# An expert stage whose blocks run as two loops per expert, with releases of their own, two gather buffers and three kinds of experts

## The reference

```python
logits = h @ w_router + b_router                 # 384 x 32
top_val, top_idx = lax.top_k(logits, 4)
gates = softmax(top_val)
for each expert e, for each block of its rows:   # xb: rows of h that chose e
    hb = xb @ w1[e] + b1[e]                      # 1024 x 2048
    glu, lin = split(hb)
    act = min(glu, 7) * sigmoid(1.702 * min(glu, 7)) * (clip(lin, -7, 7) + 1)
    y = act @ w2[e] + b2[e]                      # 1024 x 1024
    out[rows] += gate * y
```

## Time and profile before

| | |
|---|---|
| median of 3 runs | 1626.13 us |
| the profiled execution's own time | 1619.34 us |
| its span (first to last instruction) | 1617.5 us |
| PE, PEld busy | 85%, 52% |
| DVE, ACT, POOL busy | 37%, 13%, 8% |
| chain that ended last | PE 25%, DMA 23%, SP's queue 9% |
| first block of the experts, end of the span | 601.3 us, 1617.5 us |

### The profile page before, as it was taken

One profiled execution on the slowest core, in us unless ns is written; L12 is line 12 of the kernel. 1 busy time (PEld: TensorE's weight loads), 2 busy tenths in 40 slices (PEclk: granted clock), 3 DMA queues, 4 the chain that ended last, 5 costly groups with the idle time before them and its releaser, 6 DMA issues.

```text
span 1617.5 us, 47273 instructions
## 1 busy us (share of the span) xinstructions
PE 1368.3 (85%) x20097; PEld 843.9 (52%) x20098; DVE 594.4 (37%) x1172; ACT 214.3 (13%) x474; POOL 127.8 (8%) x280
## 2 busy tenths in 40 slices
PE   4899998988978959969778988768968989996965
PEld 1677666777664435525434555435534555552533
DVE  3464644787887552212112221202212221220214
ACT  0332333231302100000000000000000000000001
POOL 1000000000000011101000101001101110110100
PEclk8799999999999979979989999989989999997997
DMA  9656535000116767995999999999999999999992
GB/s 363 204 181 242 185 130 191 2 3 10 54 42 210 291 264 289 419 421 245 419 421 383 420 420 384 422 420 396 410 420 420 387 420 420 383 419 421 387 420 119
DMA packets 88379, 487.56 MB, mean 301 GB/s; under 512 B 13269, under 2 KB 15753, under 8 KB 35609
## 3 DMA queue, kind: packets, MB, share of 16 engines
q1 hardware_dynamic: 81304, 473.59, 72.4%
q10 hardware_dynamic: 3936, 6.69, 1.1%
q0 software_dynamic: 3072, 6.30, 1.1%
HBM read 481.92 MB, written 6.72 MB: 302 GB/s over the span
## 4 chain that ended last, share of the span: by engine, by line
PE 25%; DMA 23%; SPq 9%; DVE 3%; issue 2%; DVEq 0%; POOL 0%; ACT 0%
PE bank L714 25%; DMA work<-w_moe_out 9%; SPq L593 9%; DMA zbuf<-w_moe_out 8%; DMA ring<-w_moe_out 6%; DVE work L2023 1%; DVE work L2025 1%; DVE work L2024 1%; DVE ring L2044 0%; PE bank L710 0%; SPq L596 0%; DVE ring L2049 0%; SPq L628 0%; DVEq L160 0%; SPq L629 0%
## 5 line engine op out<-in xcount | busy, mean ns | idle before, releaser
L714 PE MATMUL bank<-work 128*32 128x256 f32 x5504 | 351.2, 393 | 50.5 <-DMA work<-w_moe_in 31.3
L2019 DVE TENSOR_SCALAR work<-bank 128x256 f32<-128x256 f32 x64 | 40.0, 626 | 736.8 <-PE bank L714 736.8
L714 PE MATMUL bank<-ring,work 128*32 128x256 f32 x3968 | 261.4, 393 | 43.3 <-DMA ring<-w_moe_in 25.9
L714 PEld LDWEIGHTS bank<-work 128*32 128x32 f32 x5504 | 174.0, 113 | 196.0 <-DMA work<-w_moe_in 45.3
L714 PEld LDWEIGHTS bank<-ring,work 128*32 128x32 f32 x3968 | 125.9, 113 | 144.8 <-DMA ring<-w_moe_in 35.1
L714 PE MATMUL bank<-parts 128*128 128x512 f32 (+1 forms) x720 | 168.3, 388 | 2.9 <-DVE parts L446 2.9
L714 PE MATMUL bank<-rowc 32*128 32x256 f32 (+1 forms) x2072 | 142.5, 367 | 22.6 <-issue 22.0
L710 PE MATMUL bank<-work 64*64 64x64 f32 (+3 forms) x3448 | 138.6, 233 | 15.6 <-DVE work L1751 8.5
L714 PEld LDWEIGHTS bank<-parts 128*128 128x128 f32 x720 | 129.3, 191 | 34.1 <-issue 5.2
L710 PEld LDWEIGHTS bank<-work 64*64 64x64 f32 (+2 forms) x3448 | 117.5, 136 | 34.1 <-issue 13.7
L714 PEld LDWEIGHTS bank<-rowc 32*128 32x128 f32 (+1 forms) x2072 | 87.0, 164 | 81.3 <-issue 68.7
(11 more groups left out here) (265 smaller groups left out, 1096.8 us busy)
## 6 DMA issues: line engine op xcount, KB each, us to landing
work<-w_moe_in SPq DMA_DIRECT2D x108, 1024.0 KB, 22.8
ring<-w_moe_in SPq DMA_DIRECT2D x84, 1024.0 KB, 24.9
work<-w_moe_out SPq DMA_DIRECT2D x64, 1024.0 KB, 18.1
ring<-w_moe_out SPq DMA_DIRECT2D x44, 1024.0 KB, 16.7
ring<-w_ada SPq DMA_DIRECT2D x11, 2048.0 KB, 7.5
zbuf<-w_moe_in SPq DMA_DIRECT2D x22, 1024.0 KB
first<-w_moe_in SPq DMA_DIRECT2D x21, 1024.0 KB
spare<-w_moe_in SPq DMA_DIRECT2D x21, 1024.0 KB
```

Of the source, the lines that this page charges most:

```text
L714: return pe.matmul(out, l, r, start=start, stop=stop, skip_group_check=True)
L2019: ts(in_pairs(gl), in_columns(B[0][:, 0:256]), LIMIT, None, ALU.min).then_inc(S["thd"], 1)
```

## The change

- **Two loops per expert.** PE, ACT and DVE run for each expert first `go_in` over its blocks (w1, activation) and then `go_out` (add_up, w2, copy out). On DVE and ACT these stand in a loop over the experts. The activations of an expert's blocks are kept in `zf` (12 slots of 256 columns, `act_of`); `go_out` copies one back into `act` and transposes it.
- **Releases.** w1 chunks count `mult`, w2 chunks count a semaphore of their own, `s_mul2`; SP waits for the one that belongs to the place.
- **Gathers** go into two buffers, one block further ahead. DVE first copies a gathered tile to `xs` and transposes `xT` as soon as PE is done with w1 of the block.
- **Three kinds** of experts: more than two blocks, two blocks, one block, each spread by itself, with the last one-block expert at the end. For these inputs the order becomes 0, 1, 5, 2, 8, 6, 10, 3, 11, 7, 12, 4, 17, 9, 18, 13, 20, 15, 21, 23, 14, 16, 24, 25, 22, 19, 26, 29, 28, 27, 31, 30, with 2, 2, 2, 4, 2, 1, 2, 3, 2, 1, 2, 3, 2, 1, 2, 3, 2, 1, 2, 2, 3, 1, 2, 2, 3, 1, 2, 2, 3, 1, 2, 1 blocks.
- **Small ones.** The table lists the experts of a block by a sum in which one matmul and one copy fall away; 14 small memsets write the addresses of the slots and buffers into it; PE's wait for the full lists moves behind the glu half of the first chunks, and its load of `last_it` goes.

```diff
             def multiplied(used, c):
-                sp.wait_ge(S["mult"], used * WC + (c + 1 - WC + ZQ_ALL))
+                if c < W1C:
+                    sp.wait_ge(S["mult"], used * W1C + (c + 1 - W1C + ZQ_ALL))
+                else:
+                    sp.wait_ge(s_mul2, used * W2C + (c - W1C))
...
-            last_it = gp.value_load(tab[0:1, LAST:LAST + 1], min_val=NE - 1, max_val=NBMAX - 1)
-
-            with gp.Fori(0, last_it) as it:
-                gp.wait_ge(S["xtd"], it + 1)
-                gather_listed(it)
+            last_it = gp.value_load(tab[0:1, LAST:LAST + 1], min_val=NE - 1, max_val=NBUSED - 1)
+
+            gather_listed(1, 1)
+            with gp.Fori(0, last_it + 1, 2) as it:
+                for n in range(2):
+                    gp.wait_ge(S["xtd"], it + (n + 1))
+                    gather_listed(it + (n + 2), n)
+            gp.wait_ge(S["xgd"], 16 * last_it + 48)
...
             pe.wait_ge(S["b3d"], 6)
-            pe.wait_ge(S["idxc"], 2)
-            pe.wait_ge(S["b2d"], 64)
-            last_it = pe.value_load(tab[0:1, LAST:LAST + 1], min_val=NE - 1, max_val=NBMAX - 1)
+            pe.wait_ge(S["b32"], 16 * (NB + 4))
+            pe.wait_ge(S["ohd"], 1)
...
-            def block_of(it, trio, turn_e):
+            def go_in(it, b0, trio, turn_e):
                 pe.wait_ge(S["chos"], it + 1)
+                pe.wait_ge(S["xtd"], it + 1)
                 fours(gb, selw, in_fours(b3[0:QMAX, :], 0), True, False)
-                pe.wait_ge(S["xtd"], it + 1)
...
                     else:
-                        pe.wait_ge(S["yc"], it + 1)
+                        pe.wait_ge(S["idxc"], 2)
+                        pe.wait_ge(S["yc"], b0 + 1)
+                        pe.wait_ge(S["chain2v"], 4 * it + 1)
                         fours(lb, selw, in_fours(b3[0:QMAX, :], 1), True, False)
                     for c in group:
                         fours(lb, xT[:, c, :], in_fours(place_of(turn_e, c), 1), False, c == W1C - 1).then_inc(S["mult"], 1)
+
+            def go_out(it, trio, turn_e):
+                pe.wait_ge(S["yc"], it + 1)
                 pe.wait_ge(S["ohd"], it + 1)
                 add_up(onto, ysb, it + 1)
-                pe.wait_ge(S["actd"], it + 1)
+                pe.wait_ge(S["actd"], it + 2)
                 for c in range(W1C, WC):
                     chunk_landed(trio, turn_e, c)
                     j = W2K[c - W1C]
...
+
+            def blocks_of(e, trio, turn_e):
+                b0, b1 = ended_by(e - 1), ended_by(e)
+                with pe.Fori(b0, b1) as it:
+                    go_in(it, b0, trio, turn_e)
+                with pe.Fori(b0, b1) as it:
+                    go_out(it, trio, turn_e)
 
             def ended_by(e):
-                return pe.value_load(tab[0:1, bass.ds(e + ENDS, 1)], min_val=0, max_val=NBMAX)
+                return pe.value_load(tab[0:1, bass.ds(e + ENDS, 1)], min_val=0, max_val=NBUSED)
 
...
-            add_up(onto, ysb, last_it + 2)
+                    blocks_of(e0 + i, trio, i)
+            blocks_of(NE - 2, 0, NE - 2)
+            blocks_of(NE - 1, 0, NE - 1)
+            end = ended_by(NE - 1)
+            pe.wait_ge(S["yc"], end + 1)
+            pe.wait_ge(S["ohd"], end + 1)
+            add_up(onto, ysb, end + 1)
...
+            sc.sem_inc(s_mul2, 3)
+            sc.sem_inc(S["actd"], 1)
+            sc.sem_inc(S["chain2v"], 1)
...
+            def go_in(it):
+                who = sc.value_load(tab[0:1, bass.ds(it + (WHO + 1), 1)], min_val=0, max_val=NE - 1)
                 sc.wait_ge(S["thd"], 2 * it + 1)
                 sc.activation(th, gl, ACT.Tanh, scale=ALPHA / 2).then_inc(S["thd"], 1)
-                sc.wait_ge(S["mult"], WC * it + (W1C + ZQ_ALL))
-                if not last:
-                    chosen(bass.ds(sc.value_load(tab[0:1, bass.ds(it + (WHO + 1), 1)], min_val=0, max_val=NE - 1), 1))
-                sc.wait_ge(S["mult"], WC * it + (WC + ZQ_ALL))
+                sc.wait_ge(S["mult"], W1C * it + (W1C + ZQ_ALL))
+                chosen(bass.ds(who, 1))
+
+            def go_out(it):
+                sc.wait_ge(s_mul2, W2C * it + (W2C + 3))
                 cp(ysb, B[7][:, 256:512], 0.5).then_inc(S["yc"], 1)
 
-            with sc.Fori(0, last_it) as it:
-                block_of(it, False)
-            block_of(last_it, True)
...
+            for i in range(NACT):
+                L(ve.memset(tab[:, i:NBMAX:NACT], ACTS + 256 * i))
+            for i in range(2):
+                L(ve.memset(tab[:, ROWS_AT + i:ROWS_AT + NBMAX:2], 256 * i))
...
-            L(stt(kinds[:, 1:2], nbc, 2.5, first_two, ALU.is_le, ALU.is_gt))
+            L(stt(kinds[:, 1:2], nbc, 1.5, first_two, ALU.is_gt, ALU.is_gt))
+            L(stt(kinds[:, 2:3], nbc, 1.5, first_two, ALU.is_le, ALU.is_gt))
+            L(tt(kinds[:, 1:2], kinds[:, 1:2], kinds[:, 0:1], SUB))
...
-            L(ve.memset(xg, 0.0))
+            for n in range(2):
+                L(ve.memset(xg[n], 0.0))
...
+            L(stt(keys[:, 0:2], B[5][0:NE, 4:6], 0.5, share[:, 0:2], A_, M))
+            L(stt(keys[:, 2:3], B[5][0:NE, 6:7], 1.0, share[:, 2:3], A_, M))
+            L(stt(keys[:, 0:2], keys[:, 0:2], SPREAD, kinds[:, 0:2], M, M))
+            L(tt(keys[:, 2:3], keys[:, 2:3], kinds[:, 2:3], M))
...
 
-            last_it = ve.value_load(tab[0:1, LAST:LAST + 1], min_val=NE - 1, max_val=NBMAX - 1)
-
...
-            def block_of(it, last):
+            def ended_by(e):
+                return ve.value_load(tab[0:1, bass.ds(e + ENDS, 1)], min_val=0, max_val=NBUSED)
+
+            def act_of(it):
+                here = ve.value_load(tab[0:1, bass.ds(it, 1)], min_val=ACTS, max_val=ACTS + 256 * (NACT - 1))
+                return zf[:, bass.ds(here, 256)]
+
+            def go_in(it):
...
                 in_pairs = lambda v: v.rearrange("p (c i f) -> p c f i", c=4, i=2)
+                rows = ve.value_load(tab[0:1, bass.ds(it + (ROWS_AT + 1), 1)], min_val=0, max_val=256)
+                kept = act_of(it)
                 ve.wait_ge(S["gmm"], it + 1)
                 ts(in_pairs(gl), in_columns(B[0][:, 0:256]), LIMIT, None, ALU.min).then_inc(S["thd"], 1)
                 ve.wait_ge(S["thd"], 2 * it + 2)
                 LL(stt(gg, th, 1.0, gl, A_, M))
-                ve.wait_ge(S["mult"], WC * it + (W1C + ZQ_ALL))
+                ve.wait_ge(S["xgd"], 16 * it + 32)
+                LL(cp(xs, zf[:, bass.ds(rows, 256)]))
+                ve.wait_ge(S["mult"], W1C * it + (W1C + ZQ_ALL))
+                ve.transpose(xT.rearrange("p c t -> p (c t)"), xs).then_inc(S["xtd"], 1)
                 LL(ts(in_pairs(uu), in_columns(B[7][:, 0:256]), LIMIT, -LIMIT, ALU.min, ALU.max))
-                LL(stt(act, uu, 1.0, gg, A_, M))
+                LL(stt(kept, uu, 1.0, gg, A_, M))
+                assert lchain[0] == PER
+
+            def go_out(it):
+                here = act_of(it)
+                ve.wait_ge(S["actd"], it + 1)
+                cp(act, here).then_inc(s_back, 1)
+                ve.wait_ge(s_back, it + 1)
+                ve.wait_ge(s_mul2, W2C * it + 3)
                 ve.transpose(actT.rearrange("p c t -> p (c t)"), act).then_inc(S["actd"], 1)
-                if not last:
-                    ve.wait_ge(S["xgd"], 16 * it + 32)
-                    ve.transpose(xT.rearrange("p c t -> p (c t)"), xg).then_inc(S["xtd"], 1)
                 ve.wait_ge(S["accd"], 2 * it + 4)
                 ve.wait_ge(S["idxc"], 2)
                 ts(onto, iot, slot_of[:, bass.ds(it, 1)], slot_of[:, bass.ds(it + NBMAX, 1)], ALU.is_equal, M).then_inc(S["ohd"], 1)
...
-            with ve.Fori(0, last_it) as it:
-                block_of(it, False)
-            block_of(last_it, True)
+
+            with ve.Fori(0, NE) as e:
+                b0, b1 = ended_by(e - 1), ended_by(e)
+                with ve.Fori(b0, b1) as it:
+                    go_in(it)
+                with ve.Fori(b0, b1) as it:
+                    go_out(it)
+            end = ended_by(NE - 1)
```

## The result

| | before | changed |
|---|---|---|
| median of four runs each, same chip | 1629.14 us | 1612.81 us |
| lowest to highest | 1625.94 to 1633.91 | 1609.67 to 1616.85 |
| the profiled execution's own time, its span | 1619.34, 1617.5 us | 1616.85, 1614.7 us |
| mean granted clock of TensorE | 0.941 | 0.951 |

The ratio is 0.9899, with a 95% interval of 0.9861 to 0.9937: the changed kernel is faster by 1.0%, some 16 us, where 35.5 were forecast. The time lies inside the stated range of 1580 to 1618 us, in the part of it that stood for a partial gain. The profiled execution of before was the fastest of its kernel and that of the changed kernel the slowest, so the two spans differ by only 2.8 us. The places in the traces can be compared; sizes of a few us between the two spans can't.

The account below looks back on a forecast made before the run. The stream of weight chunks was taken to bound the kernel, before and after. Start 7.0, three-block stalls 18.7, four-block expert -2.7 and end 12.5 give 35.5 us off the 1626.1 us median: 1591 us, stated range 1580 to 1618.

Parts of the forecast that it names:

- What bounds the kernel before: Expert stage: the stream of 384 weight chunks binds; stalls lose 16.8 us at the four-block expert, 18.7 at six three-block ones.
- item 3: Four-block expert, now fourth, meets a PE that is behind: 19.5 us idle in place of 16.8, so 2.7 us lost.
- the price of a block on PE: PE in the expert stage: 14.8, 28.5, 42.2 or 55.9 us for 1 to 4 blocks; 912 us, before 817.
- x: Expert stage: us that every expert costs PE beyond the price worked out; nothing much happens up to 2.0.
- slack of 2.0: Expert stage: four experts cost PE 114.0 us and the stream 121.9, leaving PE 2.0 us to spare per expert.
- the first rival: Expert stage: PE takes the stream's place, span 1529.5 + 32 x, slower from x = 2.75; chance 0.10.
- a part of the gain: Whole kernel: x between 2 and 2.75, or three-block stalls staying, gives 1602 to 1618 us; chance 0.14.
- Ahead of it DVE copies to `xs`, during w1: End of w1: DVE's copy is covered, so the next block's w1 waits only 0.64 us for the xT transpose.
- one way to x = 3.48: Handover from w1 to w2: w2 at the low clock after each pause, doubted because PE is busy some nine tenths there.
- The start: First block at 599.5 us (598.2 to 601.3), chunk 0 freed at 610.9 instead of 617.9: 7.0 us gained.
- items 3 and 4: Four-block expert loses 2.7 us standing fourth; at the end the last expert's second block goes, gaining 12.5 us.
- every jump costs: Loop entries: 32 new ones like the first, 3.41 us idle, give x = 2.8, no change; chance 0.08 with other ways.

Follow-up runs that it names:

- 11 products: Changed kernel with 11 unused 128 x 128 matmuls on PE in the pause between w1 and w2 of each expert: 1598.01 us, ratio 0.9812.
- both shortenings: Changed kernel with DVE's copy to xs ahead of the clip, and its address load not waiting for the activation product: 1595.22 us, ratio 0.9794.
- with the pause filled: Changed kernel with xs copied before the clip, the address loaded early, and 5 unused matmuls in PE's pause before w2: 1590.26 us, ratio 0.9764.

## Why the prediction was right and wrong

The sign and the places were right, the size was not: 35.5 us forecast, 16 measured.

**What bounds the kernel before** was right. The stalls of the three-block experts shrank from 18.7 to 6.7 us with the early release of w1's places, and went entirely in the runs in which PE is quicker (a share of 1.01 from 800 to 1570 us with 11 products or with both shortenings). The four-block expert's idle stretches came at 700 to 720 and 740 to 760 us, where item 3 had put them. Their size was 19.5 us in item 3: with the handover at its predicted price it is 19.2 (a share of 0.77 from 700 to 780 us in the run with both shortenings), in the changed kernel 27 (0.67), since PE is further behind there.

**The step that failed is the price of a block on PE.** 912 us were given to the 32 experts; the profiled run took 1614.7 - 17.3 - 602.6 - 0.7 = 994.1. That is x = 82.1 / 32 = 2.6 us per expert, above the slack of 2.0 from which, by the first rival, PE takes the stream's place. The slack itself was given too large: the rival's own sum, 1529.5 + 32 x, passes the forecast span of 1617.5 - 35.5 = 1582.0 at x = 1.64 already, because the 2.0 holds for stretches in which all of the stream still has to come, while the first 18 chunks, 46 us of it, are loaded ahead; the stream's idle stretches give back only a part of that. The case that came true is "a part of the gain", x between 2 and 2.75, to which I had given 0.14. The terms, each against its row:

- *Cover that wasn't there*, 29 us. "Ahead of it DVE copies to `xs`, during w1": the copy was costed at nothing, hidden by w1. It stands behind clip and tanh, which can't begin before the last part of w1, and so holds the transpose back by 0.59 - 0.14 = 0.45 us, 64 times. It is in both the restart (8.47 for 7.89, 18.5 us) and the handover (4.25 for 3.5, 24 us). Shown by the run that moves only this copy.
- *The jump and the load*: 1.18 us in the trace for the 1.0 taken, inside the bounds (0.7 to 1.5), some 6 us. The load itself was overpriced, at 0.55 us for 0.31, and the steps around it were underpriced. Lifting the wait in front saved 0.35 us of the pause. Copy, jump and load are some 35 of the 42.5 us by which restart and handover are dearer; the other 8 weren't taken apart.
- *The low clock behind each pause*, 31.2 us. It was named as "one way to x = 3.48" and dismissed, since "around the handovers it will be busy some nine tenths". The window at 875 to 885 shows PE busy 8.91 of 10 us, and yet the passes behind the pauses slow down, here the one at 903 us (granted clock 0.81 from 900 to 905). A mean over a stretch, like the 0.59 of the earlier trace rows beside 11.75 of 20 us, can't tell what a single pause does. Shown by the runs with products in the pause. The kernel before is at the low clock even more (a mean of 0.95 from 800 to 1570 us, for 0.97), but behind its waits for chunks, where the stream sets the end and not PE. The Trainium skill ("TensorE: Matmul & The Clock Gate", Part 1) says that the clock follows how busy PE has been just before; the sense agrees, and the slow passes get fewer as the pause gets shorter.

These are 18.5 + 24 + 31.2 = 73.7 of the 82.1 us; of the other 8, some 3 lie in the first expert: its second block waits 2.1 us for its rows, for 1.1 in others, and that block's w1 pass takes 9.0 us for 7.3, in part at the low clock (0.91 from 600 to 620 us). The rest I didn't take apart.

**The gains were right only in their regime.** 18.7 us of stalls and 12.5 at the end are gains of a kernel that the stream bounds. Once PE sets the end, the last block that fell away gives nothing of its own, since PE does 64 blocks in any order. The run with both shortenings bears the sum out: with PE at the predicted price the time is 1595, with the pause filled 1590, for the 1591 forecast. So the mechanism of the gains was right, and who sets the pace in this kernel was wrong; the mis-sized term is x, 2.6 us in experts of 31, where the sum needed it under 1.6. One thing stays open: the profiled stages of before and changed differ by 4 to 5 us only, the medians by 16. The profiled run of before is 10 us under its median, and no trace shows where its longer runs are longer. Its granted clock of 0.941 is also high for its kernel: in the 33 other runs for which it is on record it was 0.922 to 0.941, on the whole lower in the longer ones, which doesn't show what came first.

**The start** was right within its scatter. The 3.41 us of issue idle in the earlier trace rows are gone: in the profile the lists begin at 598.98 and the first block starts at 602.61, right behind them, where 594.50 and 601.33 stood. That the lists are 4.5 us later there (1.65 of it in the router's matmuls, 3.62 us for 1.97 at the low clock) belongs to that execution: in the second one of the same kernel the first block starts at 598.51, for the 599.5 predicted. The stream resumes at 616.76 us in the first and 611.58 in the second, for the 610.9 predicted and 617.87 before. What was missed is that the rows of the first expert's second block come too late: "the gather feeding this copy is covered too" doesn't hold there, and w1 waits 2.1 us. The memsets fitted under DVE's wait.

**The order** was mis-costed by leaving out what it does in the middle: with the slow handover it is worth 17 us in the stage and 24 in the medians, not the 12.5 - 2.7 of items 3 and 4. That it takes a slow handover to make it so large is shown.

A second rival, "every jump costs", came true at 0.6 us per entry only, as the earlier trace rows had: 19.8 us of issue idle in 31 times.

## What to carry to other kernels

A change that buys an earlier release with more work on a second resource needs that resource's price against its slack, and every "hidden" step must be placed by the time at which its inputs are there, not by the engine's idle time: here a 0.3 us copy in the wrong place of a serial chain cost 17 us of the stage, 14 between the medians. Where two resources are within 3% of each other, take the order of the work into the sum, since each part of the change is worth something else alone (8 us gained, 12 lost) than together (16 gained). And look at the clock behind each new pause of PE: if it can't be shorter, independent products in it, no longer than the pause, give the time back.

## What the runs showed of the hardware

- A pause of 2.68 us on PE, once in 30 us of work at some nine tenths busy, put 19 of 32 following passes at least in part at the low clock (5.35 us for 3.66); at 2.33 us it was 14, at 2.25 us 7, and at 1.90 us none in either of two kernels. I had not expected so steep a change.
- A product of 128 x 128 by 128 x 128 in f32 took 4.06 / 17 = 0.24 us and has two records.
- DVE's way out of one loop, into the next and through one load of an address: 1.18 us of idle, and mostly 0.80 to 0.84 between turns of the second loop. The load is a quarter of the way, as the row of DVE's sequencer in the changed kernel (shortest, median and longest of 128, in ns) shows:

```profile
L2050 DVEq TENSOR_LOAD <-tab x128: 297/305/325, 605.5 to 1592.0; - x128
```

  The Trainium skill ("DMA: Bandwidth & Descriptors", Latency and other measured facts) has a floor of about 600 ns for one tensor_load. These loads take half of that, so the floor doesn't hold here; the single one of the earlier trace rows took 0.55 us.
